# A two-block transformer kernel: the S5 recurrence on 64 chunks of 8 tokens, and a second attention with two pairs of banks

## What is computed

```python
h = _rms(x, norm1_w[l]) * (1 + sc1) + sh1
u, q, k, v = jnp.split(h @ w_in[l], [512, 1024, 1152], axis=-1)
# _s5: 32 groups of 16 channels, 64 complex states each
mag = jnp.exp(dt * lr)
a_re = mag * jnp.cos(dt * li);  a_im = mag * jnp.sin(dt * li)
bu_re = jnp.einsum("blgh,gph->blgp", ug, bb_re)      # and bu_im
# s[t] = a * s[t-1] + bu[t], complex, over all 512 tokens
y = (jnp.einsum("blgp,ghp->blgh", s_re, c_re) - jnp.einsum("blgp,ghp->blgh", s_im, c_im)
     + d_skip.reshape(32, 16) * ug)
z = jax.nn.gelu(y.reshape(bsz, seq, 512))
y_ssm = z * jax.nn.sigmoid(z @ w_glu + b_glu)
# attention: 8 query heads, 2 key heads of 64, window 128, bias by distance, one sink per head
y_attn = _swa_sink(q, k, v, rel_bias, sinks[l])
mixed = jnp.concatenate([_rms(y_ssm, out_norm_ssm[l]), _rms(y_attn, out_norm_attn[l])], axis=-1)
x = x + g1 * (mixed @ w_out[l])
```

## Time and profile before

| | |
|---|---|
| median of 3 runs | 1959.64 us (1957.53 to 1962.68) |
| profiled execution | 1957.97 us, its span 1956.1 us |
| mean granted clock of PE | 0.985 |
| PE busy | 1874.0 us (96%) |
| DVE, ACT, POOL busy | 1122.3 us, 764.0 us, 249.3 us |
| chain that ended last | PE 87%, DVE 9%, ACT 2%, issue 2% |

### The profile page before, as it was taken

The page is one execution under the profiler, slowest core; times in us unless marked ns, Lnnn a source line. Parts: engine busy times, 40 slices in busy tenths (PEclk is TensorE's granted clock), DMA queues, the critical chain, the costliest instruction groups (busy, mean ns, idle before and its releaser), DMA issues.

```text
span 1956.1 us, 22665 instructions
## 1 busy us (share of the span) xinstructions
PE 1874.0 (96%) x8169; PEld 1443.9 (74%) x8169; DVE 1122.3 (57%) x1447; ACT 764.0 (39%) x1077; POOL 249.3 (13%) x241
## 2 busy tenths in 40 slices
PE   8999999999999999999999999997787999999998
PEld 5888888878886778777888888684334768888887
DVE  6566336354555566548777333548998566556533
ACT  4222222243346866224444322333324354455422
POOL 2112001100000000031100000304674300000000
PEclk9999999999999999999999999999998999999999
DMA  6555313233221121235545222432110222223222
GB/s 203 194 172 183 117 60 105 94 115 106 87 86 65 44 65 65 87 107 179 186 141 170 86 86 91 129 108 75 54 54 11 86 65 93 100 86 95 74 88 86
DMA packets 161895, 200.57 MB, mean 103 GB/s; under 512 B 7104, under 2 KB 136490, under 8 KB 161834
## 3 DMA queue, kind: packets, MB, share of 16 engines
q1 hardware_dynamic: 148714, 163.02, 26.2%
q0 software_dynamic: 8672, 28.33, 4.4%
q10 hardware_dynamic: 4448, 8.41, 1.1%
HBM read 189.24 MB, written 10.50 MB: 102 GB/s over the span
## 4 chain that ended last, share of the span: by engine, by line
PE 87%; DVE 9%; ACT 2%; issue 2%; DMA 0%; POOL 0%; DVEq 0%; POOLq 0%; ACTq 0%
PE bank L1674 40%; PE bank L1641 34%; PE bank L1857 6%; DVE sc_a L1523 2%; PE bank L1616 2%; PE bank L1881 1%; DVE sc_v L1532 1%; PE bank L1653 1%; PE bank L1766 1%; DVE tmp L1544 1%; DVE sc_p L1544 1%; PE bank L2069 1%; DVE sc_p L1543 1%; DVE tmp L1028 1%; PE bank L1892 0%
## 5 line engine op out<-in xcount | busy, mean ns | idle before, releaser
L1012 DVE TENSOR_TENSOR w_lo<-w_raw,w_hi 128x2048 fp32r<-128x2048 f32 x157 | 369.7, 2355 | 466.3 <-ACT w_hi L615 466.1
L615 ACT CAST w_hi<-w_raw 128x2048 fp32r<-128x2048 f32 x158 | 301.3, 1907 | 757.7 <-PE bank L1674 367.5
L1674 PE MATMUL bank<-h_hi,w_hi 128*128 128x512 f32 x1120 | 448.7, 401 | 19.4 <-ACT h_hi L638 9.3
L1674 PE MATMUL bank<-h_hi,w_lo 128*128 128x512 f32 x1120 | 445.5, 398 | 0.0
L1674 PE MATMUL bank<-h_lo,w_hi 128*128 128x512 f32 x1120 | 355.3, 398 | 0.1
L1674 PEld LDWEIGHTS bank<-h_hi,w_hi 128*128 128x128 f32 x1120 | 212.6, 190 | 74.4 <-issue 22.8
L1674 PEld LDWEIGHTS bank<-h_lo,w_hi 128*128 128x128 f32 x1120 | 212.0, 189 | 52.1 <-DVE h_lo L1038 0.5
L1674 PEld LDWEIGHTS bank<-h_hi,w_lo 128*128 128x128 f32 x1120 | 212.7, 190 | 50.2 <-issue 0.2
L1641 PE MATMUL bank<-hid_hi,w_lo 128*128 128x512 f32 x528 | 208.8, 396 | 0.0
L1641 PE MATMUL bank<-hid_hi,w_hi 128*128 128x512 f32 x528 | 208.8, 396 | 0.0
L1641 PE MATMUL bank<-hid_lo,w_hi 128*128 128x512 f32 x528 | 208.8, 396 | 0.0
(11 more groups left out here) (368 smaller groups left out, 2590.6 us busy)
## 6 DMA issues: line engine op xcount, KB each, us to landing
w_raw<-in_w_in SPq DMA_DIRECT2D x29, 1024.0 KB, 5.2
mod_raw<-in_w_mod POOLq DMA_DIRECT2D x96, 256.0 KB, 3.6
w_raw<-in_ffn_w_gate SPq DMA_DIRECT2D x22, 1024.0 KB, 6.8
w_raw<-in_ffn_w_up SPq DMA_DIRECT2D x22, 1024.0 KB, 5.4
w_raw<-in_w_up SPq DMA_DIRECT2D x22, 1024.0 KB, 5.1
w_raw<-in_ffn_w_down SPq DMA_DIRECT2D x16, 768.0 KB, 4.6
w_raw<-in_ffn_w_down SPq DMA_DIRECT2D x16, 640.0 KB, 4.3
w_raw<-in_w_out SPq DMA_DIRECT2D x8, 1024.0 KB, 5.1
```

Of the source, the lines that this page charges most:

```text
L615: act.copy(w_hi[i % 2][:], w_raw[i % 2][:]).then_inc(S("w_hi_done"), 1)
L1012: dve.tensor_tensor(w_lo[s][:], w_raw[s][:], w_hi[s][:].bitcast(F32), ALU.subtract).then_inc(S("w_split"), 1)
L1674: mm = pe.matmul(bank[:], w[:, k, at], h[:, k, :], start=k == first and part == 0 and i == 0, stop=k == last and part == 1)
```

## The change

The recurrence is no longer scanned over 512 tokens but over 64 chunks of 8 tokens. What happens inside a chunk is a matrix product: a matrix from the 8 x 16 inputs of a chunk to the states at its end (`chunk_inputs`, `wb`), one from the states ahead of the chunk to its 8 x 16 outputs (`chunk_outputs`, `ca`), and one from inputs to outputs within the chunk, zero above the diagonal and with the skip term on it (`chunk_kernels`, `tz`). They are made in ffn2 and kept in DRAM:

- POOL fills `chunk_kernels` with zeros (4.46 MB) ahead of the first modulation loads, and loads the S5 matrices ahead of those of ffn2, in 20 pieces.
- Steps 0 to 7 of ffn2 are separate loops of one round. After its steps 0 to 3 DVE makes the S5 matrices, two sets of angles and the powers; after ACT's step 2 stands `rotations`, six activations and two stores for all tables, which waits for the twelfth modulation group.
- In steps 4 to 7 DVE makes two pairs of state tiles per step (`prepared`, 12 operations each), PE ends its step with `chunk_pair` twice (4 transposes, 8 matmuls with 64 rows and 16 output partitions, 4 of 16 x 16), ACT copies the results and issues 8 stores per pair (`stored`), POOL two.
- In the mixer `u2` is made with tokens on the partitions, every fourth token of 512 to a tile, by 96 matmuls; the bias turns stand between its halves. `chunk_turn` brings it into chunk form (32 matmuls), `chunk_inputs` makes the inputs of the recurrence (128 matmuls of 64 rows and 64 columns), both between the blocks of `q2`. `chunks` on DVE rotates, scans 64 steps and rotates back, for half of the states at a time, before the attention begins.
- The attention loop has two pairs of banks (0 and 1, 2 and 3) in turn. The scaling of the probabilities is one DVE operation. At units 1 to 7 `beside` puts the rest of the recurrence between the turn of a unit and its values: `within_chunks` and `from_states` (64 matmuls each, 64 rows, 128 columns), `turn_back` (64 matmuls of 64 columns), GELU on ACT and the gate product `glu` (48 matmuls).
- Behind it the norm `ps` comes first, then its half of the first two panels of `w_out2`, then `pa` and the other half.
- The rows of the eigenvalues come in 8 loads instead of 2, and the skip vector in two loads of its own.

```diff
-PHASES = {"ffn1": ((0, BESIDE_STEPS, True, 0), (BESIDE_STEPS, GU_STEPS, False, 0)),
-          "ffn2": ((0, MOD_END, True, 1), (MOD_END, BESIDE_STEPS, False, (NS - MOD_END) // (BESIDE_STEPS - MOD_END)),
-                   (BESIDE_STEPS, GU_STEPS, False, 0))}
+PHASES = {"ffn1": ((0, BESIDE_STEPS, True, None), (BESIDE_STEPS, GU_STEPS, False, None)),
+          "ffn2": (*((i, i + 1, i < MOD_END, i) for i in range(BESIDE_STEPS)), (BESIDE_STEPS, GU_STEPS, False, None))}
...
             pool.dma_start(band_dram.ap(), band[:]).then_inc(S("band_stored"), 16)
+            done(pool.memset(zero[:], 0.0))
+            flat = tz_dram.rearrange("h s t c -> (h s t c)").rearrange("(p r c) -> p r c", p=P, c=T)
+            pool.dma_start(flat, zero[:].unsqueeze(1).to_broadcast([P, CHUNK * SHIFT * 2 * NS * SG // (P * T), T])).then_inc(S("zero_stored"), 16)
...
+            for i, part in enumerate(("re", "im")):
+                for half in range(2):
+                    for k in range(4):
+                        s5_b = inp[f"ssm_b_{part}_2"].rearrange("o (k t j) n h -> k t n (o j) h", k=4, t=2)[k, half]
+                        pool.dma_start(b_in[64 * half:64 * half + 64, i, 4 * k:4 * k + 4], s5_b).then_inc(S("s5_landed"), 16)
...
+            def rotations():
+
+                act.wait_ge(S("angles_made"), 3)
+                act.wait_ge(S("mod_acc_free"), MOD_GROUPS + 1)
+                power_angles, power_sines = (tmp[:, 5, i * NS * NPOW:(i + 1) * NS * NPOW] for i in range(2))
+                for angles, sines in ((power_angles, power_sines), (angles8[:], sines8[:])):
+                    act.activation(sines, angles, ACT.Sin, scale=-TWO_PI).then_inc(S("rot_made"), 1)
+                    done(act.activation(angles, angles, ACT.Abs))
+                    act.activation(angles, angles, ACT.Sin, scale=-TWO_PI, bias=half_pi_col).then_inc(S("rot_made"), 1)
+                act.wait_ge(S("rot_made"), 4)
+                for w, table in enumerate((angles8, sines8)):
+                    act.dma_start(rot_dram[:, w, :], table[:].rearrange("p a s c -> p (a s c)")).then_inc(S("rot_stored"), 16)
+
...
-            def sw_scaled(u):
-
-                lo = P if SW_UNITS[u][0] == 0 else 0
-                act.wait_ge(S("sw_scale"), u + 1)
-                for h in range(4):
-                    p = prob[:, u % 2, h, lo:]
-                    act.activation(p, p, ACT.Copy, scale=sw_cols(80, u)[:, h:h + 1]).then_inc(S("sw_p"), 1)
...
             def sw_scale(u):
+                lo = P if SW_UNITS[u][0] == 0 else 0
+                p = prob[:, u % 2, :, lo:]
                 dve.wait_ge(S("sw_exp"), 5 * (u + 1))
...
+                done(dve.reciprocal(sw_cols(80, u), sw_cols(80, u)))
+                dve.tensor_tensor(p, p, sw_cols(80, u).unsqueeze(2).to_broadcast([P, 4, 2 * P - lo]), ALU.mult).then_inc(S("sw_p"), 1)
...
+            def chunks(half):
+
+                re, im = (B[4 + 2 * half + part][:].rearrange("p (s c) -> p s c", c=NC) for part in range(2))
+                own = slice(NS // 2 * half, NS // 2 * half + NS // 2)
+                cosine, sine = rotc[:, 0, own], rotc[:, 1, own]
+                t = [scan_t[:, i] for i in range(4)]
+                dve.wait_ge(S("bu"), half + 1)
+                if half == 0:
+                    dve.wait_ge(S("tables_landed"), 32)
+                    dve.wait_ge(S("bu"), 2)
+                    done(dve.memset(state[:, :, :, 0:1], 0.0))
+                for i, (a, w) in enumerate(((re, cosine), (im, sine), (im, cosine), (re, sine))):
+                    dve.tensor_tensor(t[i], a, w, ALU.mult).then_inc(S("scan_in"), 1)
+                dve.wait_ge(S("scan_in"), 4 * half + 2)
+                done(dve.tensor_tensor(t[0], t[0], t[1], ALU.add))
+                dve.wait_ge(S("scan_in"), 4 * half + 4)
+                done(dve.tensor_tensor(t[2], t[2], t[3], ALU.subtract))
+                for s in range(NS // 2):
+                    decay = s5[:, 20, NS // 2 * half + s:NS // 2 * half + s + 1].to_broadcast([P, NC])
+                    for i in range(2):
...
+            sw_max(0)
+            sw_max(1)
+            for u in range(len(SW_UNITS)):
+                sw_scale(u)
+                if u == 2:
+                    chunk_out(0)
+                    chunk_out(1)
+                if u == 3:
+                    chunk_out(2)
+                    chunk_out(3)
+                if u == 5:
+                    z_split(range(4))
+                if u + 2 < len(SW_UNITS):
+                    sw_max(u + 2)
...
                             mm.then_inc(S("mod_acc_free"), 1)
+                        if paired(extra):
+                            for r in range(2):
+                                chunk_pair(extra, r)
...
+            def chunk_pair(i, r):
+
+                pe.wait_ge(S("prep_step"), 12 * pair(i, r) + 12)
+                if i > MOD_END:
+                    pe.wait_ge(S("wb_turned"), pair(i, r) - 1)
+                for s in range(2):
+                    for part in range(2):
+                        at = (2 * s + part) * P
+                        pe.transpose(B[(4, 7)[r]][:, at:at + P], wb_in[:, r, s, part, :], ident[:])
+                if i > MOD_END:
+                    pe.wait_ge(S("g_read"), 4 * (i - MOD_END))
+                for s in range(2):
+                    st = 2 * pair(i, r) + s
+                    at = 2 * P * r + P * s
+                    for part in range(2):
+                        for half in range(2):
+                            own, dst = slice(64 * half, 64 * half + 64), slice(64 * half, 64 * half + SG)
+                            mm = pe.matmul(B[5][dst, at:at + P], bb[own, part, st, :], ca[own, r, part, s, 0:P],
+                                           start=part == 0, stop=part == 1)
+                            if part == 0:
+                                mm = pe.matmul(B[5][dst, at:at + SG], ident[dst, dst], skip[dst, st, :],
+                                               start=False, stop=False)
...
+            def chunk_inputs(half):
+
+                pe.wait_ge(S("tables_landed"), 32)
+                pe.wait_ge(S("u_even"), half + 1)
+                pe.wait_ge(S("u_odd"), half + 1)
+                for s in range(NS // 2):
+                    st = NS // 2 * half + s
+                    for part in range(2):
+                        for late in range(2):
+                            for t in range(2):
+                                own = slice(64 * t, 64 * t + 64)
+                                mm = pe.matmul(B[4 + 2 * half + part][own, s * NC:(s + 1) * NC], wb[own, st, part, late, :],
+                                               uc[own, st, late, :], start=late == 0, stop=late == 1)
+                mm.then_inc(S("bu"), 1)
...
+            def from_states(q):
+
+                pe.wait_ge(S("ca_landed"), 16)
+                pe.wait_ge(S("scan_out"), 2 * (q // 2) + 2)
+                for j in range(4):
+                    for part in range(2):
+                        for t in range(2):
+                            own = slice(64 * t, 64 * t + 64)
+                            mm = pe.matmul(chunk_bank(q)[own, j * P:(j + 1) * P], state[own, part, QUAD * q + j, :], ca_out[own, QUAD * q + j, part, :],
+                                           start=False, stop=j == 3 and part == 1)
+                mm.then_inc(S("o_made"), 1)
...
+            def beside(u):
+
+                if u == 1:
+                    within_chunks(0)
+                    within_chunks(1)
+                if u == 2:
+                    from_states(0)
+                    from_states(1)
+                if u == 3:
+                    for q in (2, 3):
+                        within_chunks(q)
+                        from_states(q)
+                if u == 4:
+                    for q in (0, 1, 2):
+                        turn_back(q)
+                if u == 5:
+                    turn_back(3)
+                if u == 6:
+                    for t in range(3):
+                        glu(t)
+                if u == 7:
+                    glu(3)
+
+            sw_scores(0)
+            sw_scores(1)
+            for u in range(len(SW_UNITS)):
+                sw_turn(u)
+                beside(u)
+                sw_values(u)
+                if u + 2 < len(SW_UNITS):
+                    sw_scores(u + 2)
```

More of the change, by code:

```diff
@@ L1104, in swiglu @@
                             hid_lo_of(name, i, t, 2 + t)
-                        for r in range(2, rots):
-                            turns(rotation(i, start, rots, r))
+                    if extra in range(MOD_END):
+                        setup[extra]()
                 first = 4 * MOD_AT[name]
@@ L1440, in _ @@
-            for part, (first, second, op) in enumerate(((0, 1, ALU.subtract), (1, 0, ALU.add))):
-                done(dve.tensor_tensor(t[0], b_in[:, first], f_re_b, ALU.mult))
-                done(dve.tensor_tensor(t[1], b_in[:, second], f_im_b, ALU.mult))
```

(41 more changed lines are left out.)

719 lines of the change are left out of this document (380 added, 339 removed), and 2 rows, old and new, of the table ROWS.

## The result

| | before | changed |
|---|---|---|
| median | 1959.96 us (4 runs, 1957.53 to 1962.68) | 1977.59 us (4 runs, 1976.35 to 1980.42) |
| profiled execution, span | 1957.97, 1956.1 us | 1977.67, 1976.0 us |
| granted clock | 0.985 | 0.969 |

The account below looks back on a forecast made before the run. PE was taken as the bound, except DVE in the attention loop. Terms 0.9 + 6 + 30.6 - 36 gave +1.5 on the profiled 1957.97 us: 1959.5, runs 1961, range 1936 to 1985.

Parts of the forecast that it names:

- rival B: Recurrence matmuls and pairs: row halves writing into one bank do not overlap; +18, 1979 us; chance 0.24.
- a loop above 115 us: Sign that the forecast is wrong: the second mixer's attention loop exceeding 115 us, where 102 us was expected.
- What bounds the kernel: Whole kernel: PE bounds it, with 87% of the chain; DVE's 9% are one place, the attention loop.
- The start: Kernel start: six more row loads and two for the skip vector; two issues on the path, +0.9 us (0 to 1.7).
- The zeros: Ahead of ffn1: 4.46 MB written on the queue that then loads modulation, so PE waits; +6 us (0 to 15).
- Rotations: End of ffn2's step 3: PE idles 9.6 us behind ACT's activations, stores and cast, 1.7 for clock; +11.3 us (9 to 14).
- Pairs: ffn2 steps 4 to 7: eight pairs of transposes and small matmuls on PE, 2.4 us each, +19 us (10 to 30).
- Up to the first scores: Second mixer before attention: chunk inputs and DVE's scans delay first scores from 1343.4 to 1359.2, +16 us.
- The attention loop: Second mixer: units closing through DVE, PE and ACT take 101.7 us in all, ending at 1461 against 1503.05 today.
- The ring: Attention loop: one unit closes through scale, turn, copies, values, scores and maximum, 9.9 us with the waits.
- The end: Behind the attention loop: gate, norms, half panels and whole panels take 68 us, so 1529 to 1533.
- Rival A: Zeros, pairs, loop and chunk inputs: small matmuls and stores nearly free; 1941 us; chance 0.26.

Follow-up runs that it names:

- the nine pieces: Changed kernel with the zeros written in nine pieces, one ahead of the modulation loads and one behind each ffn1 group's loads: 1970.3 us.
- the five edits: Changed kernel with scale ahead of maximum, rotations after step 3, zeros in nine pieces, pa sums behind ps sums, skip matmuls together: 1911.33 us.

## Why the prediction was right, and where it was not

The kernel came out 17.6 us slower; the forecast was +1.5, with a range to 1985 us (+25), and 0.38 on slower by over 0.3%, 0.40 on faster. So the stated range held, but the forecast's own range (1948 to 1975) did not, and that the wide range reached so far was due to rival B, whose mechanism is absent. One of the prediction's own signs of being wrong came true: a loop above 115 us. By its steps:

1. *What bounds the kernel.* Right: DVE in the loop. It is no longer without gaps.
2. *The start* (+0.9): +0.5.
3. *The zeros* (+6): +7.2, by the mechanism named; the nine pieces brought 7.3 back. The first use came at 41.4 (42 forecast).
4. *Rotations* (+11.3): 9.4 and 2.5, 11.9 (the six activations took 4.0 us for 4.5); moved, they gave 11.4 back.
5. *Pairs* (+19): +23.1, 2.9 us each instead of 2.4. The estimate went by L1996, whose matmuls have one form; the forms alternate here, and the order that avoids it is 1.1 us a pair shorter.
6. *Up to the first scores* (+16): +13.7. `chunk_inputs` took 3.9 us each instead of 5.1, `chunks` 11.4 instead of 12.3.
7. *The attention loop* (101.7 us): 116.0. This is the step that failed, a term that was mis-sized by 14.3 us, and most of the miss. The ring was the right mechanism, closed in the order written down. The parts on DVE were right (the maximum takes 3.1 us and the scale 1.6, as written). But the price of the slower clock, counted behind the zeros and the rotations, was put at nothing here without a reason: PE's parts were taken from rows at full clock, though the earlier trace rows had shown a clock of 0.90 in a loop where PE was busier than it would be now. From scale to scale units 0 to 5 took 10.2, 13.0, 14.9, 17.7, 13.3 and 19.7 us, where 7.7, 10.8, 12.6, 16.5, 12.7 and 16.0 were written: 12.5 us more in all. PE's turns, `beside` matmuls and values at the lower clock account for it, above all in unit 5 (turn 1.9 for 1.0, values 3.8 for 1.9). With DVE's order changed the loop was 88.0.
8. *The end* (68 us): 72.2. The second half panels took 14.1 us where 11.7 stood, the clock behind a wait again (the first 13.1 for 13), and the way up to the `ps` sums' end 8.7 where 7.5 stood.

Rival A did not come: the zeros and the pairs were not hidden. Its overlap of row halves is real, though. Rival B's time was nearly the measured one and its mechanism was absent; from the time alone it would have been taken for the cause.

The change itself works as it says: DVE lost 111 us in the loop, and the loop 43.6. What it brought was given back in ffn2 (+35), ahead of the loop (+14), at the zeros (+7) and at the end (+8). Most of that was order: the five edits, none of which takes work away, together give 66.3 us.

## What to carry to other kernels

When a bound engine is relieved, write down the ring of waits that remains, and ask for each engine in it whether something that is ready stands behind something that is not: here the scale of a unit behind the maximum of a later one was worth 29 us. Price PE's parts of such a ring at the clock that rows with like gaps show, not at full clock. A bulk store, a table calculation or a panel load that goes into a queue is to be priced by what stands behind it there.

## What the runs showed of the hardware

- Two matmuls of 64 rows each that write different partitions of one bank overlap: 0.055 us per record of 128 columns with both halves at a granted clock of 1.00, against 0.213 with one half at 0.50, which is an estimated 0.107 at 1.00.
- Leaving out one half of the rows lowered the granted clock in the loop from 0.79 to 0.65, with the same waits, and made the kernel 20 us slower (one run); adding 12 useless matmuls raised it to 0.82 and made the kernel 3.0 us faster.
- Four 16 x 16 matmuls between others of 64 rows cost 1.1 us more alternating than together; part of this may be the overlap of row halves.
- A store of 4.46 MB ahead of 0.26 MB loads on the same queue made the first of them take 17.2 us; the median without the store ahead is 3.5.
